# Linear attention's input products as three one-pass products over split tokens and weights, with weight tiles of 1024 columns

## The reference

```python
h = modulate(x, norm1_g, shift, scale)      # rms norm, gain, shift
proj = h @ w_in
q, k, v, r = jnp.split(proj, [GLA_DK, 2 * GLA_DK, 2 * GLA_DK + GLA_DV], axis=-1)
g = jax.nn.log_sigmoid((h @ a_w1[d]) @ a_w2[d] + a_b[d]) / GLA_GATE_NORM   # d: two directions
S_t = diag(alpha_t) S_{t-1} + k_t^T v_t;  o_t = q_t S_t                    # log alpha = g, both directions
y = (rms_norm(o, norm_g) * silu(r)) @ w_out
x = x + gate * y                            # then the FFN, which starts from x again
```

## Time and profile before

| what | value |
|---|---|
| median of 3 runs | 4294.44 us (4288.24 to 4296.98) |
| the profiled execution | 4293.35 us, its span 4291.6 us |
| PE busy, share | 3877.6 us, 90% |
| DVE busy, share | 1863.1 us, 43% |
| ACT busy, share | 1324.7 us, 31% |
| POOL busy, share | 431.7 us, 10% |
| mean granted clock | 0.939 |

### The profile page before, as it was taken

One profiled execution on the slowest core, in us unless ns is written; L12 is line 12 of the kernel. 1 busy time (PEld: TensorE's weight loads), 2 busy tenths in 40 slices (PEclk: granted clock), 3 DMA queues, 4 the chain that ended last, 5 costly groups with the idle time before them and its releaser, 6 DMA issues.

```text
span 4291.6 us, 52426 instructions
## 1 busy us (share of the span) xinstructions
PE 3877.6 (90%) x21392; PEld 3031.0 (71%) x21392; DVE 1863.1 (43%) x2812; ACT 1324.7 (31%) x1963; POOL 431.7 (10%) x277
## 2 busy tenths in 40 slices
PE   7788878999998999899978889899998888889999
PEld 3555546788886777688865667678886565767887
DVE  2544443533334434544444354543433435454433
ACT  3332322322223322333333431232232333123222
POOL 0211110000001111000021121000001122000000
PEclk9878888999998999899989999999999999999999
DMA  4112243121211221232211221033221121113232
GB/s 161 55 46 79 89 173 103 50 69 60 69 48 52 79 94 65 78 106 93 87 45 42 56 70 40 25 101 97 92 94 38 45 72 46 38 37 108 91 97 69
DMA packets 320319, 317.02 MB, mean 74 GB/s; under 512 B 8720, under 2 KB 286128, under 8 KB 319952
## 3 DMA queue, kind: packets, MB, share of 16 engines
q1 hardware_dynamic: 320080, 313.67, 23.1%
HBM read 311.55 MB, written 2.10 MB: 73 GB/s over the span
## 4 chain that ended last, share of the span: by engine, by line
PE 79%; DVE 12%; ACT 5%; issue 1%; DMA 1%; POOL 1%; DVEq 0%; SPq 0%; ACTq 0%; POOLq 0%
PE PS L132 78%; DVE scr L146 5%; ACT scr L142 3%; DVE scr L156 1%; DVE scr L164 1%; DMA ring<-in_ada_w 1%; ACT L142 1%; PE PS L135 1%; DVE NBt L156 1%; DVE scr L168 1%; DVE PS L160 0%; DVE scr L176 0%; DVE NBt L146 0%; DVE scr L172 0%; DVE ffn_h L156 0%
## 5 line engine op out<-in xcount | busy, mean ns | idle before, releaser
L132 PE MATMUL PS<-scr 128*32 128x32 f32 (+7 forms) x6692 | 662.7, 283 | 156.6 <-DVE scr L146 89.7
L132 PEld LDWEIGHTS PS<-scr 128*128 128x128 f32 (+4 forms) x6692 | 542.0, 170 | 305.2 <-issue 118.1
L132 PE MATMUL PS<-ffn_h,ffn_w 128*128 128x512 f32 (+1 forms) x3168 | 616.3, 357 | 7.8 <-DVE ffn_h L156 5.7
L132 PEld LDWEIGHTS PS<-ffn_h,ffn_w 128*128 128x128 f32 x3168 | 524.6, 189 | 100.5 <-issue 9.0
L142 ACT ACTIVATE scr<-PS 128x256 f32<-128x256 f32 (+5 forms) x425 | 193.5, 455 | 823.0 <-PE PS L132 752.9
L132 PE MATMUL PS<-h_h,ring_r 128*128 128x512 f32 (+1 forms) x976 | 357.6, 429 | 35.8 <-POOL ring_r L146 22.0
L142 ACT ACTIVATE scr<-scr 128x256 f32<-128x256 f32 (+7 forms) x404 | 212.5, 526 | 519.5 <-DVE scr L156 322.4
L132 PE MATMUL PS<-mlp_h,mlp_w 128*128 128x512 f32 x1536 | 361.3, 396 | 0.0
L132 PE MATMUL PS<-mlp_g,mlp_w 128*128 128x512 f32 x1536 | 359.7, 396 | 0.0
L132 PEld LDWEIGHTS PS<-mlp_h,mlp_w 128*128 128x128 f32 x1536 | 288.4, 188 | 70.5 <-issue 1.0
L132 PEld LDWEIGHTS PS<-mlp_g,mlp_w 128*128 128x128 f32 x1536 | 288.5, 188 | 69.9
(11 more groups left out here) (151 smaller groups left out, 4757.6 us busy)
## 6 DMA issues: line engine op xcount, KB each, us to landing
ring<-in_ada_w SPq DMA_DIRECT2D x48, 1024.0 KB, 6.1
ring<-in_ffn_w_in SPq DMA_DIRECT2D x44, 1024.0 KB, 5.1
ring<-in_w_up SPq DMA_DIRECT2D x32, 1024.0 KB, 5.4
ring<-in_w_down SPq DMA_DIRECT2D x32, 1024.0 KB, 5.0
ring<-in_w_in SPq DMA_DIRECT2D x60, 512.0 KB, 3.9
ring<-in_ffn_w_out SPq DMA_DIRECT2D x16, 1024.0 KB, 5.1
scr<-in_na_bias SPq DMA_DIRECT2D x32, 512.0 KB, 5.0
ring<-in_na_w_qkv SPq DMA_DIRECT2D x24, 512.0 KB, 4.3
```

The lines of the kernel that those rows point to most:

```text
L132: return self.eng.matmul(o, lhsT=l, rhs=r, start=start, stop=stop) if self.eng else Nothing()
```

## The change

The normed tokens are made in two float32r parts (`GH`): high where `H` was, low over `X` itself. `g_w1` is split in two parts, too. All products with the tokens (t1, q, k, v, r) become three one-pass products (`three`). A head's weights come in six tiles of 1024 columns, each in its own ring slot with its high part beside it; the low part replaces the loaded values. ACT makes the high and DVE the low part, at places written into the steps. `g_w1` is loaded first of all. Ada group 4 moves from the background into the low-rank product. The first tile of r of a head is split in the backward pass of the next head, for head 3 by a step "lead" at the end of the list. The last ada group now goes before the finish of head 3, and since the low part has overwritten `X`, the FFN reads `X` from memory again, in four transfers behind its first two weight tiles.

```diff
-    BG = [("back", 0), ("ahead", 1), ("ada", 0, 4, 7), ("back", 1),
+    BG = [("back", 0), ("ahead", 1), ("ada", 0, 5, 7), ("back", 1),
...
-          ("finish", 2), ("ada", 1, 1, 11)]
+          ("finish", 2), ("ada", 1, 1, 11), ("lead", 3)]
...
+    def g_tile(nk, *key):
+        o = ev.slot.get(key, 0) * SLOT
+        return [ringr[:, o + p:o + p + 1024].rearrange("p (k c) -> p k c", k=nk) for p in (1024, 0)]
+
+    def three(pe, o, w, k, t0, tn, first, last):
+
+        (wh, wl), (hi, lo) = w, GH
+        pe.mm(o, wh, hi[:, k, t0:t0 + tn], first, False)
+        pe.mm(o, wh, lo[:, k, t0:t0 + tn], False, False)
+        return pe.mm(o, wl, hi[:, k, t0:t0 + tn], False, last)
...
-        run(both(finish(3), ada(1, *BG_LAST)))
+        run(both(ada(1, *BG_LAST), finish(3)))
 
     def gla_sp(sp):
-        run(ada_sp(sp, 0, 0, 4))
         sp.dma(g_w1, T["gla_w1"][:, :]).then_inc(*sp.up("ld_gw1"))
+        run(ada_sp(sp, 0, 0, 5))
...
         def project(h):
-            stream(sp, ("g_qk", h), ("gla_in_full", "g_full", h, 1, 1), [(W, 0, 8, h * 128, 128), (W, 0, 8, 512 + h * 128, 128)])
-            stream(sp, ("g_v", h), ("gla_in_full", "gv_full", h, 5), [(W, 0, 8, 1024 + h * 256, 256)])
+            for q in range(2):
+                stream(sp, ("g_qk", h, q), ("gla_in_full", "g_full", h, q, 1), [(W, 0, 8, 512 * q + h * 128, 128)])
+            for e in range(2):
+                stream(sp, ("g_v", h, e), ("gla_in_full", "gv_full", h, 5), [(W, 4 * e, 4, 1024 + h * 256, 256)])
...
+            for j in range(2):
+                stream(sp, ("g_r", h, j), ("gla_in_full", "gr_full", h, j, 1), [(W, 0, 8, 2048 + h * 256 + j * 128, 128)])
...
+        run(ada_sp(sp, 1, *BG_LAST))
         finish(3)
-        run(ada_sp(sp, 1, *BG_LAST))
 
     def gla_pe(pe):
...
+        pe.wait_ge(*at("t_lo", "gw1"))
+        fill = ada_pe(pe, rg, 0, 4, 5)
+        for k in range(8):
+            next(fill, None)
+            for s, (t0, tn) in enumerate(LC):
+                pe.wait_ge(*at("nl", "g", k, s))
+                ws = slice(32 * k, 32 * k + 32)
+                t = three(pe, outs[s][0:32, 0:tn], (w1_hi[:, ws], w1_lo[:, ws]), k, t0, tn, k == 0, k == 7)
...
         def project(h):
...
+                wh, wl = g_tile(8, "g_qk", h, q)
+                pe.wait_ge(*at("g_lo_w", "g_qk", h, q))
...
+            wv = [g_tile(4, "g_v", h, e) for e in range(2)]
+            pe.wait_ge(*at("g_lo_w", "g_v", h, 1))
             for c in range(6):
...
+                    (hi, lo), (wh, wl) = gh_at(k, c * 128, 128), wv[k // 4]
+                    pe.mm(o[:, 0:256], hi, wh[:, k % 4, :], k == 0, False)
+                    pe.mm(o[:, 0:256], hi, wl[:, k % 4, :], False, False)
+                    t = pe.mm(o[:, 0:256], lo, wh[:, k % 4, :], False, k == 7)
...
     def gla_act(act):
...
+        act.wait_ge(*at("ld_gw1"))
+        act.f(w1_hi, g_w1, ACT.Copy).then_inc(*act.up("t_hi", "gw1"))
+        norm_act(act, "g", LC, ada_gain(0, 0, [0, 1])[1], gh_at)
+        run(ada_act(act, 0, 4, 5))
+        halve = lambda *key: halve_act(act, 1024, *key)
+        halve("g_qk", 0, 0)
 
         def project(h):
             z = h % 2
             for q, scl in enumerate((128 ** -0.5, 1.0)):
                 for s, (t0, tn) in enumerate((CTX, LAT)):
+                    if s == 0:
+                        halve(*(("g_v", h, 0) if q else ("g_qk", h, 1)))
...
+                if q:
+                    halve("g_v", h, 1)
...
         def inputs(h):
+            if h:
+                halve("g_qk", h, 0)
...
     def gla_dve(dve):
...
+        norm_dve(dve, "g", LC, *ada_gain(0, 0, [0, 1]), gh_at)
         for s, (t0, tn) in enumerate(LC):
             dve.wait_ge(*at("decay_full", "t1_full", s))
             dve.cp(T1[0:32, t0:t0 + tn], psum("t1", s)[0:32, 0:tn]).then_inc(*dve.up("t1", s))
+        run(ada_dve(dve, 0, 4, 5))
+
+        def halve(*key):
+            o = ev.slot.get(key, 0) * SLOT
+            dve.wait_ge(*at("t_hi", *key))
+            dve.tt(ringr[:, o:o + 1024], raw(key, 1024), ringr[:, o + 1024:o + 2048].bitcast(F32), ALU.subtract).then_inc(*dve.up("g_lo_w", *key))
+        halve("g_qk", 0, 0)
 
         def project(h):
             for q in range(2):
                 x = QK[h % 2][:, q, TC:TA]
-                for _ in range(6):
+                for n in range(6):
+                    if n == 2:
+                        halve(*(("g_v", h, 0) if q else ("g_qk", h, 1)))
                     yield
...
                 dve.tt(x, x, rtmp, ALU.add).then_inc(*dve.up("roped", "rope", h, q))
+                if q:
+                    halve("g_v", h, 1)
...
+                elif h:
+                    halve("g_r", h - 1, 0)
...
+                if n == 0:
+                    halve("g_r", h, 1)
...
     def gla_pool(pool):
...
+        pool.wait_ge(*at("t_hi", "gw1"))
+        pool.tt(w1_lo, g_w1, w1_hi.bitcast(F32), ALU.subtract).then_inc(*pool.up("t_lo", "gw1"))
...
             split.load(sp, j)
+            if i == 0 and j == 1:
+                sp.wait_ge(*at("gla_in_full", "gr_full", 3, 1, 1))
+                for k in range(0, 8, 2):
+                    sp.dma(X[:, k:k + 2, :], T["xT"][:, k * TA:k * TA + 2 * TA].rearrange("p (k t) -> p k t", k=2)).then_inc(*sp.up(f"ld_x{k}"))
...
+                        if what == "out" and i == 0:
+                            dve.wait_ge(*at(f"ld_x{k & 6}"))
                         dve.stt(x, o, gate, x, ALU.mult, ALU.add).then_inc(*dve.up("x", st, what, f0, k, s))
```

More of the change, by code:

```diff
@@ L679, in gla_bg, with gla_run @@
                 yield from finish(*a)
+            elif what == "lead":
+                lead(*a)
             else:
                 yield from ada(*a)
-    def gla_run(levels, chunks, inputs, project, gates, ready, back, finish, ada):
+    def gla_run(levels, chunks, inputs, project, gates, ready, back, finish, ada, lead):
         run(inputs(0))
@@ L928, in gla_pe @@
         att_ring, sm_ring = banks([0, 1, 2, 3]), banks([4, 5])
-        for part, _ in enumerate(gla_run(levels, chunks, inputs, project, gates, ready, back, finish, lambda i, a, b: ada_pe(pe, cur["rg"], i, a, b))):
+        for part, _ in enumerate(gla_run(levels, chunks, inputs, project, gates, ready, back, finish, lambda i, a, b: ada_pe(pe, cur["rg"], i, a, b), nothing)):
             cur["rg"] = (banks([6, 7]), banks(range(8)))[part]
@@ L1009, in back @@
                 yield
+                if n == 4 and h:
+                    halve("g_r", h - 1, 0)
                 if n < 5:
@@ L1113, in inputs @@
         def inputs(h):
-            for _ in range(3):
+            for n in range(3):
+                if n == 2 and h:
+                    halve("g_qk", h, 0)
                 yield
@@ L1340, in ada @@
                 yield
-        run(gla_run(levels, chunks, inputs, project, gates, ready, back, finish, ada))
+        run(gla_run(levels, chunks, inputs, project, gates, ready, back, finish, ada, nothing))
         pool.end("gla")
```

56 lines of the change are left out of this document (23 added, 33 removed).

## The result

| what | before | after |
|---|---|---|
| median (range, runs) | 4295.71 us (4288.24 to 4297.92, 4) | 4333.05 us (4329.67 to 4342.48, 4) |
| the profiled execution, its span | 4293.35, 4291.6 us | 4342.48, 4340.6 us |
| first product with the output weights | 696.7 us | 739.8 us |
| PE, DVE, ACT busy | 3877.6, 1863.1, 1324.7 us | 3870.0, 1897.8, 1350.9 us |
| mean granted clock | 0.939 | 0.926 |

The ratio is 1.0095, with a 95% interval of 1.0078 to 1.0113: 0.95% slower, some 37 us by the medians. I had forecast 11 us more, 4,304, and a range that ended at 4,325.

What follows compares the result with a forecast made beforehand. The prediction took the stage as bound by TensorE in places and by a chain through the other engines in others. Its terms summed to +11 us, giving 4,304 us, with own range 4,296 to 4,325 and full range 4,268 to 4,325.

Steps and rivals of the forecast that it cites:

- TensorE is the bound nearly everywhere: Rival for the whole stage: the products' saving comes off, giving 4,250, or 4,275 with half the heads' saving; chance 0.27.
- (b): Head 0: most of the 8.0 us saved on q, k and v is lost to waits for splits; -2 us.
- (d): q and k of heads 1 to 3: splits lengthen the ScalarE and VectorE chain, TensorE's saving worth nothing for head 2; +6 us.
- (e): v of heads 1 to 3: 3.0 us of new wait for a split against 3.6 saved, each; -2 us.
- (c): Ada group 4 leaves the background: about 3 us of TensorE work gone from a stretch without other cover; -3 us.
- (f): Weight ring: six slots per head instead of three make TensorE wait for ada tiles behind v; +4 us.
- (h): Stage end: r of head 3 saves 4.4, load order 1.7, the first r tile's split costs about 3; -3 us.
- Pace of the products: Three one-pass products take 0.68 us at 512 columns and 0.36 at 256; weight loads cost nothing visible.
- (a): Norm and low-rank product at the start: TensorE stands 9 us for ScalarE's row copy, then runs at low clock; +18 us.
- Two more splits per head [...] go by the same prices: Splits of each head's first q and first r tile, priced like those of q and k: ScalarE 1.06, VectorE 1.15 us.
- an idle stretch costs twice: TensorE throughout the stage: idle time costs itself and again in the work behind it, which starts at 1.2 GHz.
- (g): r of heads 0 to 2, where TensorE is the chain: 4.4 us saved less a split, net -2.2 each; -7 us.

Runs made afterwards that it cites:

- two_products: three_moves without the product of the high weights with the low tokens in q, k, v, r and the low-rank product: 4260.55 us.
- late_tr: Changed kernel with ada group 4's transposes and the rest of that group behind the low-rank product: 4321.8 us.
- no_lead: Changed kernel with head 3's first r tile split at the start of its own finish, not in a step ending the background list: 4327.94 us.
- early_v1: Changed kernel with the second v tile split right after the first, ahead of the copy of k's latent part and the rotary product: 4314.19 us.
- reorder: three_moves with the backward part of heads 1 to 3 ahead of the modulation groups, first r tile's split right behind those groups: 4292.11 us.
- reorder_before: Kernel before the change, with only the backward part of heads 1 to 3 put ahead of the modulation groups: 4292.86 us.
- last_order: Kernel before the change, with only the change's order at the stage's end, last modulation group ahead of head 3's r: 4297.28 us.
- three_moves: Changed kernel with the edits of late_tr, early_v1 and no_lead together: 4303.0 us.
- warm: three_moves with four extra unused products at each of blocks 1 to 7 of the low-rank loop: 4296.85 us.
- pool_v: three_moves with GpSimd instead of VectorE making the low parts of both v tiles of each head: 4312.76 us.
- light_ada: three_moves with modulation weight tiles from group 5 on loading two of their four blocks, read twice: 4289.74 us.
- warm_more: three_moves with reorder's order, warm's extra products and ten more ahead of k's rotary product in heads 1 to 3: 4288.71 us.

## Why the forecast was wrong

The sign and the kind of loss were right: new waits larger than the saving, with the rival "TensorE is the bound nearly everywhere" refuted by two_products (42 us for 85). The size was not. The steps that failed, first: I set the full-clock saving of v against its wait, in (b) and in (d) and (e); I charged the ring +2 for each of two heads and nothing for head 1, in (c) and (f); and I gave the late r tile of the end 3 us, in (h). Part by part:

- **Pace of the products, right.** 0.70 and 0.35 us for 0.68 and 0.36; the weight loads add nothing. The Trainium skill's rule on loads ("TensorE: Matmul & The Clock Gate", LDWEIGHTS and The mechanism) isn't borne out by these rows either.
- **(a) +18, measured +15.** Right in mechanism, down to the 9.53 us gap and the lower clock behind it; late_tr recovers 7 us of it. The gate products ran at full clock, where 2.8 us more had been charged.
- **(b) -2, measured +4.2.** Failed. From k to v it took 6.1 us where it had taken 1.7, 4.4 more where I had charged 3. v saved 1.2 us of its 3.6, its first eight triples being at the lower level, and q and k took 1.0 more.
- **A term left out, +3.7.** "Two more splits per head [...] go by the same prices", I wrote, and never added the one for the first q tile: ahead of head 1's q that split stands in ScalarE ahead of the gates' bias. But 2.4 of the 3.7 are in this one profile only: no_lead, which changes nothing here, took 39.7 us. The cost is nearer to 1.3.
- **(d) and (e), +4, measured +11.8.** Failed. Ahead of v, from first q to the start of v, the three heads took 18.7 us more, where I had 15 (6 of (d) and three waits of 3.0); the wait at v itself was forecast at 3.0 us and was 2.87 in head 2. And v saved 6.9 us where I had set 10.8 against it, at full clock, although the first paragraph of the forecast said that an idle stretch costs twice. I used that rule in (a) and forgot it here. Each is half of the miss. early_v1 takes 12.7 us from these stretches, more than they had lost.
- **(c) and (f), +1, measured +14.5** (some 12 by no_lead and late_tr). Failed by the largest amount. The waits came nearly as I had said, 2.10, 4.67 and 3.67 us behind v where I had 3 to 5. What failed is their price in the sum: I let the missing old wait pay for most of them, and the missing group 4 for head 1's, and the stretch grew there by 4.8 us all the same. TensorE's waits for modulation tiles in these three stretches went from 6.2 to 14.5 us, 8.3 more; reorder against reorder_before shows that these waits are the change's own. Another 6.6 us are longer waits for ScalarE. The split of the first r tile lies here too, which I had charged to (g), at 2.2 us a head; whether it makes these waits no run tells.
- **(g) -7, measured -8.8.** Near by luck in part. The r stretches gave 3.1 us each where the products were to give 4.4, and the split charged against them stands in the stretches above. What is right is that the saving is real where TensorE is the chain (two_products took another 7.2 us from each).
- **(h) -3, measured +2.7** (0.1 in late_tr). The 3 us for the split that waits on its load was 8.91 us at TensorE, and the 1.7 us for the order of the loads don't show (last_order). no_lead turns the stretch into a gain of 7.0.

What stays open: by the stretches of its profiled run reorder leads before by 7.4 us at the first output product, while the repeated runs put it level. The stretches of single profiles of one design differ by 3 us and more (r of head 0 took 30.4 us in last_order and 27.1 in before, with the same instructions; the end took 110.7 us in three_moves and 113.4 in warm). So the ratios are to be trusted for totals, and the stretches only for differences that recur in several kernels, as those of q to v and of r do.

## What to carry to other kernels

Price a wait together with the products behind it: where TensorE had stood for several us, the products behind it ran at half the pace for 2 to 6 us here, so a faster product type gives back part of what it saves. But subtract what the old kernel already paid there. And read the same stretch in several profiles before explaining a difference of 2 or 3 us: here the same code gave 2.81 and 5.48 us. A split or copy of tens of instructions costs little by its length (5 us for 38 us of engine time here) and much by its place: put it ahead of nothing that another engine waits for, and never ahead of a running chain when its own tile may still be on the way. Where tiles get smaller but keep a whole ring slot each, the look-ahead halves, and the loads that suffered here were those of the step behind (6.2 to 14.5 us of waiting in three stretches).

## What was not expected of the hardware

The same eight gate products, behind the same instructions, took 2.81 us in some profiles (late_tr, pool_v, light_ada) and 4.93 to 5.48 in others (three_moves, reorder): the clock level at one place can differ from execution to execution. Ten extra products ahead of a wait, with 1.91 us of it left behind them, did not lift the pace of the products after that wait (warm_more). And a GpSimd subtraction of 1024 columns, 2.43 us against VectorE's 1.23, moved off the busier engine onto one with more idle time, cost 10 us (pool_v).
